# Keys in a buffer of their own, chains in phases, ScalarE and VectorE one gather behind TensorE

## What is computed

```python
q = (xb @ wq).reshape(n, PEER_HEADS, 2, PEER_KEY_DIM)
s = jnp.einsum('nhpd,hpkd->nhpk', q, keys)
v1, i1 = lax.top_k(s[:, :, 0], 16)
v2, i2 = lax.top_k(s[:, :, 1], 16)
cand = v1[..., :, None] + v2[..., None, :]      # 256 candidates a head
top_s, pos = lax.top_k(cand, 16)                # idx: which of 16384 experts
g = softmax(top_s)
act = gelu(einsum('nhkd,nd->nhk', w_down[idx], xb))
out = einsum('nhk,nhkd->nd', g * act, w_up[idx])
```

## Time and profile before

| | |
|---|---|
| median of three runs | 3366.16 us |
| the profiled execution: its own time, its span | 3361.66 us, 3359.8 us |
| mean granted TensorE clock | 0.799 |
| PE / DVE / ACT / POOL busy | 71% / 66% / 39% / 34% |
| bytes moved by DMA, mean rate | 1288.70 MB, 384 GB/s |
| first gather issued | 313.5 us after the span's start |
| chain that ended last, by engine | PE 35%, DMA 29%, DVE 25%, ACT 5% |

### The profile page before, as it was taken

How to read it: one execution, slowest core, us unless ns; L and a number is a source line. 1 busy time by engine, 2 the same in 40 slices (tenths; PEclk the granted TensorE clock), 3 DMA queues, 4 the chain that set the end, 5 groups by cost and what they waited for, 6 DMA issues and landing times.

```text
span 3359.8 us, 38830 instructions
## 1 busy us (share of the span) xinstructions
PE 2372.6 (71%) x13176; PEld 995.5 (30%) x13176; DVE 2216.9 (66%) x5644; ACT 1295.2 (39%) x3731; POOL 1133.5 (34%) x1076
## 2 busy tenths in 40 slices
PE   6997578667775787696576695765677567756766
PEld 3445123412251235251143251341124112421111
DVE  2313855776678566738957749569957897685444
ACT  3221455345534453433433532423343333433333
POOL 0001334243434232334333433323433344334332
PEclk9998788778887888797797796886788677877666
DMA  7666999999999998999999999889999999999998
GB/s 307 238 253 232 403 383 398 388 415 406 421 415 421 401 367 351 365 415 411 412 388 389 401 418 378 332 337 385 421 392 414 422 416 388 422 416 414 421 421 363
DMA packets 170488, 1288.70 MB, mean 384 GB/s; under 512 B 19632, under 2 KB 20528, under 8 KB 24112
## 3 DMA queue, kind: packets, MB, share of 16 engines
q0 software_dynamic: 154368, 1124.14, 82.5%
q1 hardware_dynamic: 15920, 162.07, 11.7%
HBM read 1284.04 MB, written 2.10 MB: 383 GB/s over the span
## 4 chain that ended last, share of the span: by engine, by line
PE 35%; DMA 29%; DVE 25%; issue 5%; ACT 5%; POOL 0%; DVEq 0%; SPq 0%; ACTq 0%; POOLq 0%
DMA ring<-in_experts,expert 21%; PE psum L1699 11%; DVE ring L1399 9%; PE psum L1477 8%; DMA weights<-in_chunks 7%; DVE arena L1288 6%; PE psum L1463 6%; PE psum L1647 3%; PE psum L1435 1%; PE psum L1512 1%; DMA ring<-in_chunks 1%; PE psum L1449 1%; PE psum L1610 1%; PE psum L1594 1%; ACT diag L1017 1%
## 5 line engine op out<-in xcount | busy, mean ns | idle before, releaser
L1699 PE MATMUL psum<-ring,diag 64*64 64x512 f32 x8192 | 1373.2, 786 | 684.8 <-ACT diag L1017 681.4
L755 POOL DMA_INDIRECT ring<-in_experts,expert x1024 | 1107.8, 1082 | 1954.9 <-PE psum L1699 1816.6
L1399 DVE CUSTOM_DVE_ANT_0 ring<-ring,h 128x1024 f32<-128x1024 f32 x1024 | 1225.2, 1223 | 592.1 <-DMA ring<-in_experts,expert 571.9
L1699 PEld LDWEIGHTS psum<-ring,diag 64*64 64x64 f32 x8192 | 296.9, 161 | 1592.8 <-ACT diag L1017 1354.5
L1015 ACT ACTIVATE acts<-dots 128x1 f32<-128x1 f32 x1024 | 205.9, 201 | 1372.0 <-DVE dots L1399 1357.7
L1477 PE MATMUL psum<-arena,weights 128*128 128x128 f32 x2048 | 293.9, 312 | 140.4 <-DMA weights<-in_chunks 140.4
L1017 ACT ACTIVATE diag<-ident_half,shares_of 128x64 f32<-128x64 f32 x1024 | 356.0, 348 | 33.3
L1477 PEld LDWEIGHTS psum<-arena,weights 128*128 128x128 f32 x2048 | 282.3, 225 | 189.5 <-DMA weights<-in_chunks 158.9
L1016 ACT ACTIVATE shares_of<-acts,gate 128x1 f32<-128x1 f32 x1024 | 301.7, 295 | 33.4
L1288 DVE SCALAR_TENSOR_TENSOR arena<-kept,taps,arena 128x128 f32<-128x128 f32 x960 | 263.3, 345 | 2.3
L781 ACT ACTIVATE arena<-psum 128x512 f32<-128x512 f32 (+1 forms) x105 | 65.8, 626 | 324.1 <-PE psum L1477 236.5
(11 more groups left out here) (182 smaller groups left out, 1633.6 us busy)
## 6 DMA issues: line engine op xcount, KB each, us to landing
weights<-in_chunks SPq DMA_DIRECT2D x68, 2048.0 KB, 11.6
ring<-in_chunks POOLq DMA_DIRECT2D x46, 1024.0 KB, 5.7
ring<-in_experts,expert POOLq DMA_INDIRECT x1024, 12.8
weights<-in_chunks SPq DMA_DIRECT2D x15, 512.0 KB, 10.0
ring<-in_chunks SPq DMA_DIRECT2D x2, 2048.0 KB, 16.5
x<-in_x SPq DMA_DIRECT2D x1, 2048.0 KB, 14.2
kept<-in_chunks POOLq DMA_DIRECT2D x2, 1024.0 KB, 18.2
out_x<-x SPq DMA_DIRECT2D x4, 512.0 KB, 11.7
```

Source lines behind the costliest of these rows:

```text
L755: pool.indirect_dma_start(out=ring[:, k, :], out_offset=None, in_=table, in_offset=bass.IndirectOffsetOnAxis(ap=expert[:, s.b % 2, n:n + 1 ...
L1399: dve.tensor_tensor_reduce(out=ring[:, k, 0:D], in0=ring[:, k, 0:D], in1=h2[:, s.b % 2, :], scale=1.0, scalar=0.0, op0=ALU.mult, op1=ALU.a ...
L1699: pe.matmul(ffn_out[rows_out, r * COLS:(r + 1) * COLS], diag[rows_in, k, :], ring[rows_in, k, D + n * COLS:D + (n + 1) * COLS], start=Fals ...
```

## The change

- **Keys.** The key halves no longer take one of the two buffers. They go to 4 KB a partition of the arena (`key_half`), loaded from SP's queue in their place in the list; the first half after the norm's h_t is ready, the second after scores(1), which is the last reader of the first. `pq_t` shrinks to two quarters, and select's order becomes: project 0, project 1, scores 0, project 2, scores 1, project 3, scores 2, a phase with nothing, scores 3. Top-k starts at phase 5 (block 0's first select keeps the old order, and phase 3).
- **Chains split.** norm gets a phase more (ScalarE's squares and root, then VectorE's scaling, then TensorE's transposes). q heads have 6 phases in place of 3, attend 23 in place of 13 (exps and mix apart from score and turn, squares and root apart from the end), conv 34 in place of 17 (one tap a phase, not two; two phases between statistics and scaling). gating and conv keep their standard deviation in std_v and rstd_v. peak, expsum and inv_sum have a place for each head.
- **Costs and orders.** The phases' costs are changed, and the even mixer's phases of different stages are interleaved by a written list, `EVEN`, in place of three moves in `phases_of`.
- **LOOK is 1.**

```diff
-LOOK = 2
+LOOK = 1
...
             for c in s.needs.get(phase, ()):
+                if c.after:
+                    self.keys_loaded += 16
+                    c.landed = self.keys_loaded
+                    self.chunks.append(c)
+                    continue
...
-        s = Stage("norm", ..., cost=(2, 4, 3) if dest else (2, 4))
+        s = Stage("norm", ..., cost=(1.2, 5.5, 5.5, 3) if dest else (1.2, 5.5, 5.5))
...
-        s = Stage("conv", b=b, cost=(5.4,) * len(TAP_RUNS) + (5, 4))
+        s = Stage("conv", b=b, cost=(2.7,) * len(TAP_RUNS) + (2.5, 2, 5, 5))
...
-        s = Stage("select", layer=layer, b=b, cost=(4.2, 4.2, 2) + (3,) * (5 * QUARTERS))
+        s = Stage("select", layer=layer, b=b, first=first, cost=(3.6,) * (3 if first else 5) + (3.2,) * (5 * QUARTERS))
...
+        s.keys = [self.key((layer * 2048 + half * 1024, layer * 2048 + (half + 1) * 1024), s.s[1] if half else ("ht_ready", s.ht))
+                  for half in range(2)]
...
-ATTEND = [("score", 0), ("score", 1), ("turn", 0), ("out", 0), ("score", 2), ("turn", 1), ("out", 1), ("score", 3), ("turn", 2),
-          ("out", 2), ("turn", 3), ("out", 3), ("end", 0)]
+ATTEND = [("score", 0), ("exps", 0), ("mix", 0), ("score", 1), ("exps", 1), ("mix", 1), ("turn", 0), ("score", 2), ("exps", 2),
+          ("out", 0), ("mix", 2), ("turn", 1), ("score", 3), ("exps", 3), ("out", 1), ("mix", 3), ("turn", 2), ("out", 2), ("turn", 3),
+          ("out", 3), ("squares", 0), ("root", 0), ("end", 0)]
...
+SELECT = [("linear", 0, 0), ("linear", 0, 1), ("linear", 1, 0), ("linear", 1, 1), ("scores", 0, 0), ("linear", 2, 0), ("linear", 2, 1),
+          ("scores", 1, 0), ("linear", 3, 0), ("linear", 3, 1), ("scores", 2, 0), ("wait", 0, 0), ("scores", 3, 0)]
...
-TAP_RUNS = [(lo, lo + 2) for lo in range(1, TAPS, 2)]
+TAP_RUNS = [(lo, lo + 1) for lo in range(1, TAPS)]
...
-        pq_t = at(2048, 2048).rearrange("p (g n) -> p g n", g=2 * PH)
+        pq_t = at(2048, 1024).rearrange("p (q g n) -> p q g n", q=2, g=PH // 2)
+        key_half = at(3072, 1024)
...
+                if c.after:
+
+                    if isinstance(c.after, Tile):
+                        sp.wait_ge(full[c.after.bank], c.after.full_after[0])
+                    else:
+                        sp.wait_ge(S[c.after[0]], c.after[1])
+                    sp.dma_start(key_half, A["chunks"][c.source, :, c.cols[0]:c.cols[1]]).then_inc(keys_landed, 16)
+                    return
...
             def conv(s):
                 for _ in TAP_RUNS:
                     yield
+                yield
                 act.wait_ge(S["var_ready"], s.var + 1)
-                signal("std_ready", act.activation(std[:, 0:1], meanvar[:, 1:2], ACT.Sqrt, bias=eps[:]))
+                signal("std_ready", act.activation(std_v[:], meanvar[:, 1:2], ACT.Sqrt, bias=eps[:]))
+                yield
                 yield
...
                 for what, h in ATTEND:
-                    if what == "score":
+                    if what == "exps":
                         exps(h)
...
-                for what, h in ATTEND[:-1]:
+                for what, h in ATTEND[:-3]:
                     if what == "score":
                         peaks(h)
-                    elif what == "turn":
+                    elif what == "mix":
                         combine(h)
                     yield
```

More of the change, by code:

```diff
@@ L280, in attend @@
     def attend(self, b):
-        s = Stage("attend", b=b, cost=tuple({"score": 4, "turn": 2.5, "out": 2.5, "end": 4}[what] for what, h in ATTEND))
+        s = Stage("attend", b=b, cost=tuple(ATTEND_COST[what] for what, h in ATTEND))
         s.qkt, s.v = self.so_far("qkt_ready"), self.so_far("v_ready")
@@ new lines, with written @@
+p3 p4 p5
+"""
+TAP_RUNS = [(lo, lo + 1) for lo in range(1, TAPS)]
+def written(stages, words):
+    order = [(stages[word[0]], int(word[1:])) for word in words.split()]
+    for s in stages.values():
+        assert [n for t, n in order if t is s] == list(range(len(s.cost))), s.kind
+    return order
+def phases_of(makers):
+    order = []
+    for make in makers:
+        made = make()
+        order += made if isinstance(made, list) else [(made, n) for n in range(len(made.cost))]
+    return order
@@ L472, in even, with mixer @@
     def even(b):
[L473 to L474 removed]
+        def mixer():
+            norm = p.norm(("x", b), None, ("one", 0), (0, SH1))
+            stages = {"n": norm, "q": p.heads("q", [b + CTX // P], Q_CH), "g": p.gating(b), "a": p.attend(b), "p": p.project(b, "even")}
+            return written(stages, EVEN)
+        return [mixer] + ffn_prep(0, b)
     def pointwise(b):
```

200 lines of the change are left out of this document (121 added, 79 removed).

## The result

The changed kernel took a median of **3454.86 us** in four runs (3444.64 to 3461.60), the kernel before 3366.36 in four: a ratio of 1.0268, 95% interval 1.0238 to 1.0297, so 88 us slower, where the prediction had 3301 us, 60.5 us faster than the profiled execution of before. The profiled execution took 3461.6 us, with a span of 3459.8 and a mean granted clock of 0.772, against 3361.66, 3359.8 and 0.799. The median lies outside the predicted range, 3250 to 3345, and 62 us above even the slower rival's 3393.

A forecast was written before the change was run, and what follows sets the result against it. The DMA engines bound the kernel, losing 155.4 us where the ring runs dry. Terms −34.4 − 6.1 − 17 − 11 + 8 = −60.5 us took 3361.7 to 3301 us, range 3250 to 3345, forecast chance 0.50.

The forecast's parts named there:

- slower rival: All hand-overs to TensorE: LOOK 1 gives up 185 us of cover, half of it bare costs 92 us; 3393 us, chance 0.10.
- Part 1: Select: keys in their own place end the weight waits, lost bytes fall from 49.4 to 15 us; −34.4 us.
- half comes back: Select: second key half late, or VectorE's top-k becomes the limit; keys give some 10 us, not 34; 3325 us, chance 0.19.
- waits for weights under 30 us: Sign of being right: TensorE's waits for weights in select fall from 140 us to under 30.
- select over 400 GB/s: Sign of being right: select windows in blocks 2 and 4 rise from 374 and 355 to over 400 GB/s.
- Part 2: Attend: phases of a head stand one or more slots apart, lost bytes fall from 11.1 to 5 us; −6.1 us.
- Turn finds its data: Attend: TensorE's turn no longer waits for VectorE's combine, the reason given for the −6.1 us.
- Part 3: Convolution to projection: shorter tap runs and split statistics remove two of three TensorE idle stretches; −17 us, bounds −40 and 0.
- Part 4: Norms, q heads, gating and block 0's attend in more phases win back under half their loss; −11 us, bounds −25 and 0.
- Part 5: conv_in in blocks 2 and 4 gets fewer slots because other stages spread, losing more bytes; +8 us, bounds 0 and +11.
- Part 6: Before the first gather: TensorE's order changes by a few phases, nothing is removed; 0, bounds ±4 us.
- The argument against: Against the slower rival: TensorE idles over 800 us in blocks 0 to 6, its chains long because of the second slot.

The follow-up runs named there:

- the run with the old order: Changed kernel with LOOK 2, select put back to its old order and old costs in every block: 3338.10 us, ratio 0.9916.
- its front and its select mended: Changed kernel with LOOK 2, exps moved directly behind score in the front for two heads, and select's old order and costs: 3332.42 us, ratio 0.9897.
- two other kernels: LOOK 1 for LOOK 2 on the kernel with keys and convolution changed, 3397.55 us, and on the kernel before, 3497.12 us.

## Why the prediction was wrong

Two steps failed. The larger is the price of the shorter lead: the sum charged it 1.09 us on each of four SiLUs, 4.4 us in all, and it measured 97 us. The other is what the new order and the extra phases cost: select's later top-k was put at nothing and measured 20 to 31 us, and parts 2 and 4 were credited with 17 us and brought none. Without the first (LOOK 2) the time is 3358 us, still 57 us over the forecast.

*Part 1, keys:* right for the keys by themselves, wrong for the change. −34.4 us was forecast for select's bytes; alone the keys took 34 off them and 40 off the time (part of it in the front, which the prediction had not counted on). The rival's late second key half never came: no wait for it in any trace. But the change also moved select's order, which the prediction read as the frame for the keys' gain and costed at nothing. Its later top-k makes VectorE the bound at select's end; that costs 31 us in one setting and, taken back, returns 20 in another. The prediction had this as the second condition of its rival "half comes back" (VectorE's top-k takes over), and saw VectorE "near" its limit in select, but gave the new order no term in the sum. Together with the crowding of the run with the old order, it leaves select at 61 us lost with LOOK 2, more than the 55 of before. The mark "waits for weights under 30 us" was met (0.0) while "select over 400 GB/s" was not (381 and 354). The wait was a true cost, and others took its place.

*Part 2, attention:* −6.1 us forecast. The row attend falls from 18 to 13 us in the full change with LOOK 2, but that is the window's end: with the even projection, in which its last phases now stand, it goes from 16 to 22. Done alone, attend's lost bytes fell by 1 and the whole was 11 us dearer. The step that failed is "Turn finds its data", taken for the cause of the lost bytes: turn does find its data, and the bytes stay lost. What loses them stays open.

*Part 3, convolution:* right at LOOK 2 for the convolution. −17 us forecast, 20 measured, with costs of 2.2 a tap run where the change has 2.7. In the changed kernel itself, with LOOK 1, that row falls by 7 us.

*Part 4, norms, heads, gating:* −11 us forecast, not found. The changed kernel with LOOK 2, its front and its select mended, is at 3332, 9 us over the keys alone, although the convolution's 20 us are in it. Attention's 11 us are part of that; norms, heads and gating were not run alone, and the front's first gather, 12 us later than with the keys alone, is in it too.

*Part 5, density:* conv_in with LOOK 2 loses 12 us in its two blocks together where it lost 10; +8 was too much. With LOOK 1 it loses 41.

*Part 6, the front:* 0 ± 4 forecast, 16.9 us measured (313.5 to 330.4). The bounds were drawn from "nothing is removed", but a split chain gets later at each part where the list puts other evacuations between them. Taking back a part of it (exps moved forward for two heads) returned 9 us; that the rest has the same cause is not shown.

*The lead:* here the sign was lost. The forecast charged LOOK 1 once, as one gather's 1.09 us on each of four SiLUs, and left the rest to the rival with a chance of 0.10. The rival's mechanism was right: 185 us of cover given up, half of it bare, 92 us; measured 97, or 94 and 131 on two other kernels. That the size came so near is luck in part, for the half was assumed and not worked out, and the lead turned out to be worth nothing in select, which the count did not set apart. Its condition was that over a third lies bare, and the rows already spoke for it: TensorE waited 353 times for diag with two gathers in hand, and the 3.50 and 4.23 us of the earlier trace rows are idle time on top of that cover. A wait that stands in spite of a cover says that the cover is used up there, so a gather taken off it lengthens the wait by that gather, wherever the ring does not hold it. The argument against, that the chains were long because of the second slot, has something in it, since LOOK 3 adds 19 us; but from 2 to 1 the lost cover outweighs it by far.

Added up by single runs: keys −40, convolution −20, select's order +31, attention +11 and LOOK 1 +97 make 3366 + 79 = 3445, 10 us under the 3455 measured. The terms come from different kernels (select's order is 31 us on one and 20 on another, the lead 94 to 131), so the sum closes to some 10 or 20 us and no better; what is left holds the front and the other splits, which were not run alone.

## What to carry to other kernels

Where in-order engines share one list, the lead of one over the others is a buffer like any other: count the loop from its phase through the others and back (here about 4 us) and compare it with the work in hand (1 to 2 us a gather). If the engine already waits with the present lead, expect a shorter one to cost much of what it takes away, stage by stage: in select it cost nothing here. And a large change with one term of each sign should be run in parts: here two of them were worth 63 us (3366 to 3304), and the rest spent 151.

## What the runs showed of the hardware

The same matmuls take longer or shorter with TensorE's clock. The gathers' matmuls in the page of before:

```profile
L1699 PE MATMUL psum<-ring,diag 64*64 64x512 f32 x8192 | 1373.2, 786 | 684.8 <-ACT diag L1017 681.4
```

The same 8192 took 1499.3 us after, at a granted clock of 0.772 for 0.799: 126 us of busy time more without one matmul more. A gather's eight took 1.09 us in places and 1.91 to 1.98 in others, nearly the two to one of the clock's levels (2.4 and 1.2 GHz). LOOK 1 raised this busy time in each of three pairs (1373 to 1438, 1452 to 1499 and 1443 to 1482 us). But it is no measure of the time: the kernels with the keys alone and with keys and convolution have 1428 and 1443 us of it and are faster than before. Which gaps lower the clock was not tried by itself. The Trainium skill, "TensorE: Matmul & The Clock Gate", Part 1, says that the throttled state is the default and that activity releases it; this trace agrees as far as the clock is lowest of the stages above, 0.60, in one that is VectorE's, the convolution of block 4 (125 of 155 us busy), and 0.96 in conv_in, where TensorE works for 85 of 94.

The same 0.5 MB of keys landed in 7.8 us in the arena and in 10.0 us as chunks of the buffers; why was not tried. The 2 MB loads took 11.9 and 11.6.
